# The first turning of the retention's rows, moved from step 1 to step 3 of a turn

## The reference

```python
scores = jnp.einsum('bhcnd,bhcmd->bhcnm', qc, kc) * decay_mask[None, :, None]
y_inner = jnp.einsum('bhcnm,bhcme->bhcne', scores, vc)
...
y = (y_inner + y_cross).reshape(B, H, S, D)
mu = jnp.mean(y, axis=-1, keepdims=True)
var = jnp.mean(jnp.square(y - mu), axis=-1, keepdims=True)
y = (y - mu) * lax.rsqrt(var + EPS)
y = y.transpose(0, 2, 1, 3).reshape(B, S, H * D)
return (jax.nn.silu(g.astype(jnp.float32)) * y).astype(q.dtype)
```

## Time and profile before

| | us |
|---|---|
| median of 3 runs | 648.96 |
| lowest, highest | 647.77, 649.9 |
| the profiled execution | 648.42 |
| its span in the trace | 646.6 |
| TensorE busy | 634.9 |
| VectorE busy | 380.7 |
| ScalarE busy | 298.4 |
| GpSimd busy | 72.0 |

### The profile page before, as it was taken

One profiled execution on the slowest core, in us unless ns is written; L12 is line 12 of the kernel. 1 busy time (PEld: TensorE's weight loads), 2 busy tenths in 40 slices (PEclk: granted clock), 3 DMA queues, 4 the chain that ended last, 5 costly groups with the idle time before them and its releaser, 6 DMA issues.

```text
span 646.6 us, 9380 instructions
## 1 busy us (share of the span) xinstructions
PE 634.9 (98%) x3210; PEld 527.4 (82%) x3210; DVE 380.7 (59%) x565; ACT 298.4 (46%) x485; POOL 72.0 (11%) x88
## 2 busy tenths in 40 slices
PE   7999999999999999999999999999999999999996
PEld 7888878878888877899888888888888888878885
DVE  3457558648757767876555555555555644473455
ACT  5557348537636736555333333333333433353341
POOL 5413103103111203230000000000000000000002
PEclk9999999999999999999999999999999999999999
DMA  9644223333321546641433333333333023422313
GB/s 280 187 131 131 66 65 98 98 97 97 98 61 69 189 139 195 190 136 46 118 97 97 97 97 97 97 97 97 98 91 103 31 67 98 162 65 66 97 65 130
DMA packets 87398, 70.20 MB, mean 109 GB/s; under 512 B 2297, under 2 KB 76201, under 8 KB 87378
## 3 DMA queue, kind: packets, MB, share of 16 engines
q1 hardware_dynamic: 85906, 64.67, 33.0%
q0 software_dynamic: 1472, 5.26, 2.8%
HBM read 67.81 MB, written 2.12 MB: 108 GB/s over the span
## 4 chain that ended last, share of the span: by engine, by line
PE 95%; DMA 1%; ACT 1%; POOL 1%; DVE 1%; issue 0%; SPq 0%; DVEq 0%; POOLq 0%; ACTq 0%
PE bank L439 85%; PE bank L582 2%; PE bank L570 1%; PE bank L519 1%; DMA raw<-in_w_in_dram 1%; PE bank L510 1%; PE bank L560 1%; PE bank L509 1%; PE bank L559 1%; PE bank L450 1%; POOL ws L364 1%; ACT ws L774 0%; ACT hT L781 0%; PE bank L546 0%; PE bank L535 0%; PE bank L496 0%
## 5 line engine op out<-in xcount | busy, mean ns | idle before, releaser
L439 PE MATMUL bank<-hT,ws 128*128 128x512 f32 (+1 forms) x1872 | 409.7, 375 | 1.3 <-DVE hT L1074 0.8
L439 PEld LDWEIGHTS bank<-hT,ws 128*128 128x128 f32 x1872 | 328.9, 188 | 62.0 <-DVE hT L1074 1.5
L439 PE MATMUL bank<-ws,yT 128*128 128x512 f32 x720 | 166.7, 390 | 0.3 <-PE bank L439 0.3
L439 PEld LDWEIGHTS bank<-ws,yT 128*128 128x128 f32 x720 | 134.3, 188 | 28.4 <-issue 1.1
L1058 DVE TENSOR_TENSOR ws<-raw,ws 128x1024 fp32r<-128x1024 f32 x85 | 103.5, 1218 | 6.9 <-ACT ws L774 6.4
L774 ACT ACTIVATE ws<-raw 128x1024 fp32r<-128x1024 f32 x88 | 92.6, 1053 | 15.4 <-PE bank L439 11.5
L1342 DVE TENSOR_TENSOR ws<-raw,ws 128x1024 fp32r<-128x1024 f32 x22 | 26.9, 1224 | 51.2 <-ACT ws L1018 51.2
L995 ACT ACTIVATE gains<-bank,conv 128x512 f32<-128x512 f32 x22 | 17.1, 779 | 75.0 <-PE bank L439 75.0
L1018 ACT ACTIVATE ws<-raw 128x1024 fp32r<-128x1024 f32 x22 | 23.3, 1057 | 56.2 <-PE bank L439 56.2
L995 ACT ACTIVATE rot<-bank,conv 128x512 f32<-128x512 f32 x22 | 17.1, 779 | 67.7 <-PE bank L439 67.7
L1319 DVE SCALAR_TENSOR_TENSOR gains<-bank,conv,gains 128x511 f32<-128x511 f32 x22 | 16.5, 749 | 52.8 <-ACT gains L995 52.8
(11 more groups left out here) (111 smaller groups left out, 479.5 us busy)
## 6 DMA issues: line engine op xcount, KB each, us to landing
raw<-in_w_up_dram SPq DMA_DIRECT2D x44, 512.0 KB, 3.8
raw<-in_w_in_dram SPq DMA_DIRECT2D x28, 512.0 KB, 4.0
raw<-in_w_down_dram SPq DMA_DIRECT2D x22, 512.0 KB, 3.8
raw<-in_w_out_dram SPq DMA_DIRECT2D x16, 512.0 KB, 4.1
xs<-in_x_dram SPq DMA_DIRECT2D x6, 512.0 KB, 4.2
work<-bias_vectors POOLq DMA_DIRECT2D x4, 512.0 KB, 4.1
work<-in_decay_dram POOLq DMA_DIRECT2D x4, 512.0 KB, 4.7
out_dram<-work SPq DMA_DIRECT2D x4, 256.0 KB, 2.1
```

The costliest lines, as they stand in the source:

```text
L439: return nc.tensor.matmul(dst, st, mv, start=start, stop=stop)
```

## The change

Three things move within `mixer_turn`, in turns 1 to 3. On TensorE, `ret_rows` goes from the visit of step 1 to that of step 3, where it stands ahead of the turning of the first pair's probabilities. On VectorE, `ret_center` goes from step 2, ahead of the second pair's maxima, to step 4, behind the second pair's normalising. On ScalarE the square goes from step 3 to step 4, behind the copies of the first pair's turned probabilities. What is computed is the same, and the waits are the same ones.

```diff
@@ TensorE, mixer_turn
-                    if u == 1 and not first:
+                    if u == 3 and not first:
                         ret_rows(i - 1)
@@ ScalarE, mixer_turn
                         exponent(u)
-                    if u == 3 and not first:
-                        act.wait_ge(r_centered, i)
-                        nc.scalar.activation(squares, centered, ACT.Square).then_inc(r_sq, 1)
                     if u in (4, 6, 8, 10):
                         copy_turned(u - 4)
                         copy_turned(u - 3)
+                    if u == 4 and not first:
+                        act.wait_ge(r_centered, i)
+                        nc.scalar.activation(squares, centered, ACT.Square).then_inc(r_sq, 1)
@@ VectorE, mixer_turn
                         normalise(i, u - 1)
-                    if u == 2 and not first:
+                    if u == 4 and not first:
                         ret_center(i - 1)
```

## The result

The changed kernel took 651.33 us (median; 650.94 to 653.01), the kernel before 648.82 in the same comparison. The ratio is 1.0038, with a 95% interval of 1.0025 to 1.0052: 2.5 us slower, 1.6 to 3.4 by the interval. The forecast was 651.3, in a range of 648.8 to 653.6, and slower with a chance of 0.55.

The account below looks back on a forecast made before the run. TensorE, busy 634.9 of 646.6 us, bounds the kernel. Terms 0.04 + 0.65 + 0.10 = 0.79 us a turn, 2.4 in three turns, took 648.42 to 650.8; 0.54 for the median gave 651.3, range 648.8 to 653.6.

Parts of the forecast that it names:

- TensorE's part: Visit at step 1 removed, visit at step 3 lengthened: +0.04 us a turn, bounds -0.05 and +0.10.
- The centring at E: VectorE, turn 1: E is the end of the moved centring, put at 100.74 us, where it was 94.73.
- The square, the copy and the exponentials: ScalarE: square waits for the centring, weight copy and third pair's exponentials queue behind; second exponential ends 103.84, was 101.77.
- The order at the port: Shared VectorE/GpSimd port: rotary sum, asked for 0.05 us before L1058, goes first; L1148 ends at 107.33 us.
- rival B: L1058 gets the port before the rotary sum; waits 0.64 and 0.53, 1.21 us a turn, 652.6 us; chance 0.17.
- The two waits: TensorE waits 0.65 us a turn before L535 (rows' second turning) and 0.10 before unit 6's first matmul.
- the gate: Unit 6's first matmul overwrites the bank that gating L1153 reads; slack 0.76 us, wait put at 0.10 a turn.
- A: The forecast itself: the rotary sum goes ahead of L1058; 0.79 us a turn, 651.3 us; chance 0.45.
- The signs: Profile marks naming the course, such as sum or L1058 lengthened; L1148 ending before 106.7 us would refute the forecast.
- Rival C: Not slower: L1058 and the rotary sum run beside each other at usual lengths; 649.3 us; chance 0.25.
- step 9: Turning of third pair's probabilities, seen as 0.0 to 0.5 us from waiting; part of a 655 us rival, chance 0.08.

Follow-up runs that it names:

- run 1: The changed kernel with ScalarE's weight copy L774 ahead of the square: ratio to the kernel before 0.9997, turns of 53.01 and 53.04 us.
- Run 8: The changed kernel with six small useless VectorE instructions ahead of L1058 (the weights' low part): ratio 1.0052, turns of 53.66 and 53.67 us.
- run 7: The kernel before with four small useless VectorE instructions ahead of L1058: 650.41 us in one execution, turns of 53.20 us.
- run 9: The changed kernel with four small useless VectorE instructions ahead of L1058: 652.76 us in one execution, turn 1 54.78 us, turn 2 53.74.
- run 5: The changed kernel with the rotary sum ahead of the power on GpSimd: ratio 1.0027, turns of 53.40 us.

## Why the prediction was right, point by point

- **TensorE's part is nothing.** Right: -0.03 us a turn (+0.04 forecast; the bounds were -0.05 and +0.10). Step 2 came 0.48 us earlier, where 0.40 was worked out.
- **The centring at E.** From step 1's start it ended after 100.15 - 90.07 = 10.08 us; 100.74 - 90.59 = 10.15 was forecast.
- **The square, the copy and the exponentials.** The mechanism was right, and run 1 shows it as the cause; the size was off. From the square's start to the second exponential's end it took 102.77 + 0.19 - 100.18 = 2.78 us, not 3.03. Where nothing is waited for, the copy and the first exponential are written as starting 0.09 us before the end of the one ahead (100.72 and 101.67, for ends at 100.81 and 101.76), which the sum didn't take off for the copy. And the 2.41 us taken from the earlier trace rows had some waiting in it: from the copy's start to the exponential's it is 0.95 us here and was 1.11 before, where the exponential began 0.04 after its maximum was there (100.43):

```profile
100.47 0.62 ACT L883 ACTIVATE xs<-xs,negmax 128x384 f32<-128x384 f32 x1
```

- **The order at the port.** This is the step that failed. L1058 came 13.46 us after step 1's start instead of 13.81, the sum 13.67 instead of 13.76, so L1058 was 0.21 ahead instead of 0.05 behind, and went first. Of the 0.35 us that L1058 came earlier, 0.25 are ScalarE's chain and 0.07 the centring. The course was rival B's, which had a chance of 0.17.
- **The two waits.** The wait before L535 was 0.35 us, not 0.65 (B: 0.64), as L1148 ended 0.36 earlier with the exponentials. The one at the gate was 0.67, not 0.10; rival B had 0.53. With TensorE's -0.03 that is 0.99 of the 1.01 a turn, between A's 0.79 and B's 1.21.
- **The signs.** Those of B came: the long sum (2.16 us, 2.4 named) and idle time before unit 6's first matmul put down to L1153 (0.41). L1148's end at 106.45 lies under the 106.7 that was to refute the forecast, but turn 1 began 0.5 us earlier: from step 1's start it is 16.38 us, against 106.7 - 90.59 = 16.11, so the sign wasn't met.
- **The total.** 2.4 us were forecast; three turns give 3.0 and the comparison of times 2.5, with an interval that holds both. That the median came out at the forecast to the tenth is luck in good part: the first wait was put 0.30 us too high and the second 0.57 too low, and the loss by the traces is a quarter larger than the sum. Run 8, in A's order, is 0.78 us a turn over the kernel before, where A's sum had 0.79, but in other parts: 0.80 before L535 and nothing at the gate, for 0.65 and 0.10.
- **Rival C** (both beside each other) is shown wrong: in no run did the sum and a whole L1058 run side by side at their usual lengths. The row that spoke for it was misread: at 103.56 the sum was written as starting with 0.14 us of L1058 left, but it ended at 104.85, 1.15 after L1058's end, just as in the earlier trace rows and in the changed kernel. So it had waited there as well, within its 1.29 us.

No run was clearly faster than the kernel before. The trace of the kernel before notes no wait of TensorE in the turns, so by these traces this change could give no more than the 0.03 us a turn of the merged visit.

## What to carry to other kernels

When a step moves later in a hand-written order, follow its queue neighbours, not only its own results: here a square that had been early became the head of a queue, and what cost most of the time (0.87 of 1.01 us, run 1) was the weight copy and the attention's exponentials behind it. Work out every place where the busy engine meets the delayed chain, not only the first, since the second (the gate) and the third (step 9) were less than 0.8 us behind. Where two engines ask for one port within some tenths of a microsecond, give both orders a price, and don't take a lead of 0.05 us for certain: here the order was worked out wrong by 0.26.

## What the runs showed of the hardware

A VectorE instruction with two inputs in SBUF and GpSimd's sum (L392, two inputs in SBUF) never ran together: the sum ended 1.15 or 1.16 us after the instruction that held it up, and VectorE's of 128x512 ended 0.55 after the sum. The Trainium skill says so too (page "SBUF — State Buffer", section "Who interferes with whom"), and adds that the one that issues first has the pair. The second half is not the whole of it here. Asked for 0.21 us after L1058's start (the changed kernel), the sum had its turn before L1148; asked for 0.79 after it (run 7), it had to let L1148 go first; and in turn 1 of run 9 it was asked for 0.08 us before L1059's written start and was passed by two instructions. GpSimd's power on 128x8, 1.68 us long, held nothing up: L1058 took its usual 1.22 us beside it. What decides the order at a handover is left open.

Two inputs are not needed for it: VectorE's TENSOR_SCALAR, with one tensor input in SBUF (the normalising has a 128x1 factor beside it, the small instructions none), was held up by the sum as well. The normalising of 128x256 took 1.42 us beside it for 0.35 alone (run 5, and turn 0 of the kernel before), and one small instruction of 128x8 took about 1.3, where such ones start 0.07 apart otherwise (run 8). So it isn't only L1058 and L1148 that have to be kept clear of the sum.
